# Whole-expert loads in a mixture-of-experts step: one 3 MB load each from the eighth round of three on, with smaller splits around it

## The chip, the core and the metric

The kernel runs on one NeuronCore of one Trainium2 chip. The metric is the device time of one execution in microseconds, as the median of several runs. All data is float32. The engines are TensorE (PE; PEld is its weight load), VectorE (DVE), ScalarE (ACT), GpSimd (POOL) and SyncE (SP), which here does little else than issue DMAs.

## What is computed

Two layers of a backbone over 256 tokens of width 1024: 128 context tokens and 128 latent ones. Each layer has token mixers (retention, differential attention, latent attention), and then a mixture of experts:

```
def trunk_layer(x, cond, lw, ...):
    shift1, scale1, gate1, shift2, scale2, gate2 = split(silu(cond) @ w_ada + b_ada)
    h = rmsnorm(x, norm_mix) * (1 + scale1) + shift1
    x = x + gate1 * (token_mixers(h) @ w_out)
    h = rmsnorm(x, norm_ffn) * (1 + scale2) + shift2
    return x + gate2 * moe_ffn(h)

def moe_ffn(h):    # 64 experts, top 6 of them per token, ff = 256
    eidx, gates = route(sigmoid(h @ router_w) + router_bias)     # grouped top-k
    routed = sum over a token's 6 experts e of gates_e * (silu(h @ w_gate[e]) * (h @ w_up[e])) @ w_down[e]
    return routed + (silu(h @ sh_gate) * (h @ sh_up)) @ sh_down
```

An expert has 2 MB of gate and up weights (each 1 MB) and 1 MB of down weights. Every expert is computed, so both layers read 2 x 64 x 3.1 MB = 403 MB of expert weights.

## The kernel before

**Rounds.** After the mixers of a layer come 22 rounds over the 64 experts: two rounds with two experts each (the fixed ones), then 20 rounds of three, numbered 0 to 19 here (`TRIOS = 20`). "Round r" below is always round of three number r, and the eighth of them is round 7. Experts are sorted by how many tokens chose them; a round has 128 places, 64 for a big expert and 32 for each of two small ones.

**One round on TensorE** (`expert_round`, L2216) in its fixed order: gates and up (L2228, 128 matmuls, waits for `gates_in`), the first half of the gather of the next round's tokens (L2155), the scatter of the previous round's results into the sum in PSUM (L2162), the transposes of hidden values and gated choice (L1642), the second half of the gather, and the down matmuls (L2264, waits for `downs_in`). It counts up `gate_done`, `up_done` and `down_done`. ScalarE copies down results to `yy` in two halves (L1048, `results`). Round 2 has the shared expert's up matmuls in between, round 4 its down matmuls (`sh_down`). In the last round the scatter of round 18's results lies beside the gates and ups, and its own results are scattered behind the downs. VectorE then adds the sum to the residual `xT` (L1610), the norm of the next layer follows.

**Buffers.** Six places for gate and up weights, A, B, C_, D_ (the ring `gu`), F (`fifth`) and S_ (`sixth`, the memory of the hidden tokens), and six for down weights. From round 6 on even rounds use A, B, D_ and odd rounds C_, F, S_, so the loads of round r+2 go where round r's were. The first six rounds have an order of their own (`BUFFERS`, L569).

**Loads** are all issued by SyncE, in program order, on one queue, with waits in between. For round r+2 it reads three expert numbers (`expert_in`), waits for `up_done` of round r, issues the three gate and up loads of 2 MB (L630), waits for `down_done` of round r and issues the three down loads of 1 MB (L633). The last round's gates and ups are six loads of 1 MB (L627). From `trio_loads` (L777), which rounds 6 to 19 use:

```
x = [expert_in(sp, l, at(trio_at(r) + n)) for n in TAKES]
sp.wait_ge(S["up_done"], m * 2 + (r0 + r + 1))
if last: ... load_halves_to(r, js, x, half)
else: load_to(r, js, x)
sp.wait_ge(S["down_done"], m * 2 + (r0 + r + 1))
load_dn_to(r, js, x)
```

In it, r is the round that is loaded, and the counts are those of round r-2. Ahead of it (L774) SyncE waits for `sh_down`, then loads the third down weights of round 5. For rounds 1 and 2 it waits once for `up_done` of round 0 (L738) and issues loads of whole gate and up blocks. The next layer's first weights go into the ring's places as these come free, in an order fixed at L447.

**In HBM** `exp_w_both` holds an expert's gate and up weights as 128 rows of 16 KB, `exp_w_down` its down weights as rows of 8 KB. The residual norm is `norm` (L848 on ScalarE).

## Time and profile before

| | us |
|---|---|
| median of 3 runs (lowest, highest) | 1324.35 (1323.11, 1327.59) |
| the profiled execution, device time | 1323.6 |
| its span, first to last instruction | 1321.7 |
| PE busy | 1218.5 (92%) |
| PE weight loads busy | 835.3 (63%) |
| DVE busy | 280.8 (21%) |
| ACT busy | 239.4 (18%) |
| DMA, mean rate over the span | 376 GB/s |

The page's slices, 40 of 33 us each; a digit is a busy share in tenths, PEclk the granted TensorE clock in tenths of full speed:

```profile
PE   6999999999998898888989999999999888988896
PEclk8999999999998898999999999999999999999999
DMA  9779849999999999999966653999999999999994
GB/s 397 317 311 362 338 181 422 398 427 423 410 424 426 426 427 424 427 427 426 420 266 250 250 225 150 415 417 425 424 397 427 424 428 424 426 427 427 423 423 173
```

Slices 7 to 20 and 26 to 40 are the rounds of the two layers. Times are from the span's start. In the views that follow, an idle time in square brackets stands before an instruction, with what ended it; the chain of waits gives start, duration and what was waited for or ran; a DMA's duration in it is from issue to landing. The view by windows has, for each window, busy time and count of PE, PEld, DVE, ACT and POOL, the granted clock, the DMA share, and GB/s.

### The profile page before, as it was taken

What the parts mean: (1) busy time and instruction counts of PE and PEld (TensorE: products, weight loads), DVE (VectorE), ACT (ScalarE), POOL (GpSimd) and SP (SyncE); (2) the same over time, 40 slices, a digit from 0 to 9 for tenths busy, and PEclk for the clock granted to TensorE, in tenths of its full rate; (3) what the DMA queues carried; (4) which work ended last, traced back from release to release, by engine and by line L of the source; (5) the groups of instructions that cost most, each with busy time, mean ns of one, the idle gap of its engine ahead of it and who ended that gap; (6) DMA issues with size and microseconds to landing.
All of it is one profiled execution on the core that took longest, in us unless ns stands there. A gap on an engine that the chain in (4) does not pass through costs nothing.

```text
span 1321.7 us, 25818 instructions
## 1 busy us (share of the span) xinstructions
PE 1218.5 (92%) x11196; PEld 835.3 (63%) x11196; DVE 280.8 (21%) x720; ACT 239.4 (18%) x533; POOL 2.8 (0%) x13
## 2 busy tenths in 40 slices
PE   6999999999998898888989999999999888988896
PEld 4566687676765565656665658866766564656564
DVE  1252362101011010101034425511111010101012
ACT  2353132101010110000134521411010101100112
POOL 0000000000000000000000000000000000000000
PEclk8999999999998898999999999999999999999999
DMA  9779849999999999999966653999999999999994
GB/s 397 317 311 362 338 181 422 398 427 423 410 424 426 426 427 424 427 427 426 420 266 250 250 225 150 415 417 425 424 397 427 424 428 424 426 427 427 423 423 173
DMA packets 50937, 496.82 MB, mean 376 GB/s; under 512 B 8752, under 2 KB 9008, under 8 KB 10160
## 3 DMA queue, kind: packets, MB, share of 16 engines
q1 hardware_dynamic: 46800, 493.75, 89.8%
q10 hardware_dynamic: 4064, 2.00, 0.5%
q8 instruction: 57, 0.93, 0.3%
q14 instruction: 16, 0.13, 0.0%
HBM read 493.73 MB, written 2.00 MB: 375 GB/s over the span
## 4 chain that ended last, share of the span: by engine, by line
PE 52%; DMA 40%; DVE 3%; SPq 2%; issue 1%; ACT 1%; DVEq 0%; ACTq 0%
DMA xh<-in_exp_w_both 31%; PE PS L2228 16%; PE PS L1732 7%; DMA dn<-in_exp_w_down 4%; PE PS L2064 4%; PE PS L2155 4%; PE PS L2264 4%; PE PS L2162 3%; PE PS L1674 2%; DMA arena<-in_exp_w_both 2%; DMA gu<-in_exp_w_both 2%; PE PS L2113 1%; DMA gu<-in_w_in_wide 1%; PE PS L1642 1%; PE PS L1855 1%
## 5 line engine op out<-in xcount | busy, mean ns | idle before, releaser
L2228 PE MATMUL PS<-gu,arena 128*32 128x256 f32 (+1 forms) x4000 | 334.3, 398 | 72.4 <-DMA gu<-in_exp_w_both 35.2
L2228 PEld LDWEIGHTS PS<-gu,arena 128*32 128x32 f32 (+1 forms) x4000 | 193.7, 116 | 217.5 <-issue 89.2
L2228 PE MATMUL PS<-arena 128*32 128x256 f32 (+1 forms) x768 | 181.8, 397 | 0.0
L2155 PE MATMUL PS<-arena 128*128 128x128 f32 x1408 | 176.3, 278 | 0.5 <-ACT arena L1065 0.5
L2155 PEld LDWEIGHTS PS<-arena 128*128 128x128 f32 x1408 | 164.0, 192 | 18.3 <-issue 17.2
L2264 PE MATMUL PS<-dn,arena 128*32 128x512 f32 (+1 forms) x976 | 160.1, 595 | 2.7 <-DMA dn<-in_exp_w_down 2.7
L2162 PE MATMUL PS<-arena 128*128 128x256 f32 x704 | 160.2, 380 | 1.4 <-ACT arena L1048 1.4
L2264 PE MATMUL PS<-arena 128*32 128x512 f32 (+1 forms) x368 | 152.1, 595 | 0.0
L2162 PEld LDWEIGHTS PS<-arena 128*128 128x128 f32 x704 | 130.2, 190 | 20.7 <-ACT arena L1048 3.2
L2228 PE MATMUL PS<-xh,arena 128*32 128x256 f32 x608 | 139.7, 402 | 0.0
L1558 DVE TENSOR_TENSOR arena<-arena,PS 128x256 f32<-128x256 f32 x44 | 18.5, 422 | 548.3 <-ACT arena L1061 548.3
L1048 ACT ACTIVATE arena<-PS 128x512 f32<-128x512 f32 x88 | 52.6, 597 | 373.5 <-PE PS L2264 373.5
L2264 PEld LDWEIGHTS PS<-dn,arena 128*32 128x32 f32 (+1 forms) x976 | 40.9, 111 | 82.7 <-issue 74.8
L2228 PEld LDWEIGHTS PS<-arena 128*32 128x32 f32 (+1 forms) x768 | 88.6, 117 | 0.0
L1061 ACT ACTIVATE arena<-PS 128x256 f32<-128x256 f32 x44 | 16.9, 384 | 382.8 <-PE PS L2228 382.8
L1552 DVE COPY arena<-PS 128x512 f32<-128x512 f32 x44 | 30.4, 691 | 209.8 <-PE PS L1642 209.8
L2228 PEld LDWEIGHTS PS<-xh,arena 128*32 128x32 f32 x608 | 66.0, 116 | 2.7
L1732 PE MATMUL PS<-gu,xh 128*128 128x512 f32 (+1 forms) x160 | 51.7, 478 | 0.0
L1732 PE MATMUL PS<-xh,gu 128*128 128x256 f32 x192 | 44.6, 392 | 1.8 <-DVE xh L1159 1.8
L1732 PEld LDWEIGHTS PS<-xh,gu 128*128 128x128 f32 x192 | 37.1, 196 | 10.7 <-issue 5.3
L1732 PEld LDWEIGHTS PS<-gu,xh 128*128 128x128 f32 x160 | 26.7, 190 | 21.8 <-issue 21.3
L1674 PE MATMUL PS<-gu,condw 128*32 128x512 f32 x320 | 38.1, 598 | 0.1
(264 smaller groups left out, 1021.7 us busy)
## 6 DMA issues: line engine op xcount, KB each, us to landing
gu<-in_exp_w_both SPq DMA_DIRECT2D x76, 2048.0 KB, 25.4
dn<-in_exp_w_down SPq DMA_DIRECT2D x84, 1024.0 KB, 26.4
arena<-in_exp_w_down SPq DMA_DIRECT2D x44, 1024.0 KB, 27.8
gu<-in_w_ada_pieces SPq DMA_DIRECT2D x20, 2048.0 KB, 8.8
arena<-in_exp_w_both SPq DMA_DIRECT2D x20, 2048.0 KB, 27.7
xh<-in_exp_w_both SPq DMA_DIRECT2D x14, 2048.0 KB, 34.2
gu<-in_exp_w_both SPq DMA_DIRECT2D x20, 1024.0 KB, 14.2
gu<-in_w_in_wide SPq DMA_DIRECT2D x8, 2048.0 KB, 14.2
```

The lines of the kernel that those rows point to most:

```text
L1048: return A(yy[:, :, half], PS[:, 7 - n, :].rearrange("p (t c) -> p c t", c=NC_), ACT.Copy)
L1061: A(sact, PS[:, 5, 0:FF], ACT.Silu).then_inc(S["silu_ready"], 1)
L1552: return v.tensor_copy(turned_back, PS[:, 6, :])
L1558: tt(hh, sact, PS[:, 5, FF:2 * FF], ALU.mult).then_inc(S["hid_ready"], 1)
L1642: return pe.transpose(dst, src, ident[0:parts, 0:parts])
L1674: ins = mmul(PS[32 * j:32 * j + 32, 7, :], condw[:, 2 * quarter + c, :], wv[:, c, 512 * j:512 * j + 512], start=(quarter == 0 and c == 0), ...
L1732: ins = mmul(PS[0:lhs(k).shape[-1], bank, o:o + rhs(k).shape[-1]], lhs(k), rhs(k), start=(k == 0), stop=(k == NC_ - 1))
L2064: ins = mmul(PS[:, wo_bank(c), (c % 2) * T:(c % 2) * T + T], wo[k // 4][:, k % 4, c], mixT[:, k] if k < 4 else latent_T[:, k - 4], start=( ...
L2155: ins = mmul(PS[:, 4, (c % 4) * P:(c % 4) * P + P], h_tok[:, g, c], onehot[b][:, g], start=(g == 0), stop=(g == 1))
L2162: ins = mmul(PS[:, c // 2, (c % 2) * T:(c % 2) * T + T], yy[:, c], selT, start=(first and c % 2 == 0), stop=False, skip_group_check=True)
L2228: ins = mmul(PS[w * h:w * h + w, 5, FF * half:FF * half + FF], xg[:, k, w * h:w * h + w], weights[half][:, k], start=(k == 0), stop=(k == ...
L2264: ins = mmul(PS[w * h:w * h + w, 7 - n, :], hidT[:, j * P + w * h:j * P + w * h + w], weights[:, j, 512 * n:512 * n + 512], start=(j == 0) ...
```

## The change

- Gate, up and down weights of an expert stand together in HBM (`exp_w`, 128 rows of 24 KB), with the down weights in two halves of 512 columns. On the chip each ring place holds gate, up and down weights side by side; F too. `dn` becomes a list of four views of the ring. S_'s down weights use `fourth_dn`, and D_'s from round 6 on the ring's own place.
- `trio_loads`, rounds 7 to 18: an expert is one 3 MB load after `down_done` of round r-2. Only S_, the third of an odd round, keeps a 2 MB load after `up_done` and a 1 MB load.
- Round 6 is written out: its gates are asked for before the waits for `sh_down` and `down_done`, and round 5's third down weights after both.
- Rounds 1 and 2: gate halves after `gate_done` of round 0, up halves after `up_done`.
- The last round: its down weights come in two column halves with a semaphore for each; results go to the scatter and the residual by column halves.
- ScalarE's square root table is asked for ahead of the squares in layer 2 as well; the slots of the next layer's first weights change order.

```diff
-        gu = sb("gu", [P, RING, 2 * NC_ * FF])
-        dn = sb("dn", [P, RING, 2, D])
+        ring = sb("ring", [P, RING, 2 * BLOCK + 2 * D])
+        gu = ring[:, :, 0:2 * BLOCK]
+        OWN = (3, 1, 0, 2)
+        dn = [ring[:, slot, 2 * BLOCK:].rearrange("p (j n) -> p j n", j=2) for slot in OWN]
...
-                    slot = n if l == 0 else expert_slot[l - 1][(0, 1, 3, 2)[n - starts[l]]]
+                    slot = n if l == 0 else expert_slot[l - 1][(3, 0, 1, 2)[n - starts[l]]]
...
+            def load_dn_half(j, l, x, half, told):
+                at = half * D
+                sp.dma_start(dn_place(j)[:, at:at + D], down(l, x)[:, at:at + D]).then_inc(S[told], 16)
+            def load_whole(j, l, x, told):
+                sp.dma_start(fifth_whole if j == F else ring[:, expert_slot[l][j], :], expert(l, x)).then_inc(S[told], 16)
...
-                sp.wait_ge(S["up_done"], r0 + 3)
-                load_to(1, (A,), x1[2:])
-                load_to(2, (B,), x2[:1])
-                load_half(D_, l, x2[1], 0, "even_in")
-                load_fourth_up(l, x2[1], "even_in")
+                for half in range(2):
+                    sp.wait_ge(used[half], r0 + 3)
+                    load_halves_to(1, (A,), x1[2:], half)
+                    load_halves_to(2, (B,), x2[:1], half)
+                    if half == 0:
+                        load_half(D_, l, x2[1], 0, "even_in")
+                    else:
+                        load_fourth_up(l, x2[1], "even_up_in")
...
+                x6 = experts(6, 0, 1, 2)
+                sp.wait_ge(S["up_done"], r0 + 7)
+                load_to(6, (A, B, D_), x6)
                 sp.wait_ge(S["sh_down"], l + 1)
+                sp.wait_ge(S["down_done"], r0 + 7)
                 load_dn_to(5, (S_,), x5[2:])
+                load_dn_to(6, (A, B, LATE_D), x6)
...
+                    if r % 2:
+                        sp.wait_ge(S["up_done"], m * 2 + (r0 + r + 1))
+                        load(S_, l, x[2], "odd_in")
                     sp.wait_ge(S["down_done"], m * 2 + (r0 + r + 1))
-                    load_dn_to(r, js, x)
+                    for j, xj in zip(buffers(r), x):
+                        if j == S_:
+                            load_dn(S_, l, xj, "odd_dn_in")
+                        else:
+                            load_whole(j, l, xj, ("even_in", "odd_in")[r % 2])
+                def last_loads(r):
+                    x = experts(r, 0, 1, 2)
+                    sp.wait_ge(S["up_done"], r0 + r + 1)
+                    for half in range(2):
+                        load_halves_to(r, buffers(r), x, half)
+                    sp.wait_ge(S["down_done"], r0 + r + 1)
+                    for half, told in enumerate(("odd_dn_in", "last_dn_in")):
+                        for j, xj in zip(buffers(r), x):
+                            load_dn_half(j, l, xj, half, told)
...
-                if k % 2:
+                if k > 0:
                     A(small[:, 500:501], col("eps"), ACT.Sqrt)
...
-                    half = slice(64 * n, 64 * n + 64)
-                    return A(yy[:, :, half], PS[:, 7 - n, :].rearrange("p (t c) -> p c t", c=NC_), ACT.Copy)
+                    return A(yy[:, 4 * n:4 * n + 4], PS[:, 7 - n, :].rearrange("p (c t) -> p c t", c=4), ACT.Copy)
...
                     for n in range(2):
+                        if last and n == 1:
+                            pe.wait_ge(S["last_dn_in"], 48 * l + 48)
                         for j in range(2):
                             for h, weights in enumerate(dns):
                                 ins = mmul(PS[w * h:w * h + w, 7 - n, :], hidT[:, j * P + w * h:j * P + w * h + w],
-                                           weights[:, j, 512 * n:512 * n + 512], start=(j == 0), stop=(j == 1))
+                                           by_half(weights)[:, n, j], start=(j == 0), stop=(j == 1))
...
-                pe.wait_ge(S["y_out"], 2 * (r0 + ROUNDS))
-                scatter(told=S["combined"])
+                for half in range(2):
+                    pe.wait_ge(S["y_out"], 2 * (r0 + ROUNDS) - 1 + half)
+                    scatter(told=S["combined"], cs=range(4 * half, 4 * half + 4))
...
+    down = named["exp_w_down"].reshape(DEPTH, E, P, 2, 2, D // 2)
+    named["exp_w_down"] = down.swapaxes(3, 4).reshape(DEPTH, E, P, 2 * D)
+    named["exp_w"] = np.concatenate([named.pop(f"exp_w_{n}").reshape(DEPTH, E, P, 2 * D) for n in ("gate", "up", "down")],
+                                    axis=-1)
```

TensorE's waits follow: an even round from 8 on waits for three whole loads before its gates, an odd one for S_'s gates and two whole loads.

## Rows read from the trace of the kernel before

**Rows 1.** View by windows, two whole rounds of layer 2.
```profile
1072.20:1116.50 44.30, 38.23 (x424) 25.18 (x425) 4.95 (x10) 4.35 (x8) 0.00 (x0) 0.96 1.01 426
```
**Rows 2.** Chain of waits, rounds 15 to 19 of layer 1: start, us, what.
```profile
565.84 8.84 PE PS L2228 x128
...
575.89 34.10 DMA xh<-in_exp_w_both
...
610.12 8.80 PE PS L2228 x128
...
626.59 3.62 PE PS L2264 x32
...
630.36 1.77 SPq L633
...
663.08 3.67 PE PS L2264 x32
```
**Rows 3.** Timeline of PE, from round 18's gates to round 19's, layer 1.
```profile
632.26 7.11 PE L2228 MATMUL PS<-gu,arena 128*32 128x256 f32 x128 [2.10 <-DMA gu<-in_exp_w_both]
...
646.97 0.63 PE L2264 MATMUL PS<-dn,arena 128*32 128x512 f32 x3
...
650.43 0.39 PE L2228 MATMUL PS<-gu,arena 128*32 128x256 f32 x2
```
**Rows 4.** Timeline of PE, the gates of round 8, layer 1.
```profile
410.76 9.97 PE L2228 MATMUL PS<-gu,arena 128*32 128x256 f32 x128 [3.73 <-DMA gu<-in_exp_w_both]
```
**Rows 5.** Last round of layer 2: PE and DVE timelines, then the chain of waits.
```profile
1289.69 0.39 PE L2228 MATMUL PS<-gu,arena 128*32 128x256 f32 x2
...
1301.25 0.69 DVE L1552 COPY arena<-PS 128x512 f32<-128x512 f32 x1 [1.07 <-PE PS L1642]
...
1302.64 0.14 issue
1302.78 3.67 PE PS L2264 x32
...
1307.13 1.15 PE PS L2162 x4
```
**Rows 6.** DMA issues at 197.98, 243.13, 249.69, 250.21: KB each, us to landing.
```profile
arena<-in_exp_w_both SPq DMA_DIRECT2D x1, 2048.0 KB, 14.1
...
arena<-in_exp_w_down SPq DMA_DIRECT2D x1, 1024.0 KB, 8.6
...
gu<-in_exp_w_both SPq DMA_DIRECT2D x1, 2048.0 KB, 7.6
...
gu<-in_exp_w_both SPq DMA_DIRECT2D x1, 2048.0 KB, 13.4
```
**Rows 7.** Windows before an issue at 185.59; that load's landing; the page's y_prompt store.
```profile
180.00:185.50 5.50, 5.50 (x27) 4.85 (x26) 3.43 (x10) 1.05 (x2) 0.00 (x0) 1.00 0.01 1
...
gu<-in_exp_w_both SPq DMA_DIRECT2D x1, 2048.0 KB, 7.7
...
out_y_prompt<-arena ACTq DMA_DIRECT2D x1, 512.0 KB, 3.1
```
**Rows 8.** View by windows, the stretches in which loads run dry.
```profile
245.00:255.00 10.00, 10.00 (x119) 7.63 (x112) 0.42 (x1) 0.98 (x2) 0.00 (x0) 1.00 0.91 352
345.00:350.00 5.00, 5.00 (x49) 2.77 (x52) 2.05 (x4) 0.60 (x1) 0.00 (x0) 1.00 0.98 342
885.00:890.00 5.00, 5.00 (x73) 3.63 (x66) 0.42 (x1) 0.38 (x1) 0.00 (x0) 1.00 1.02 397
980.00:990.00 10.00, 10.00 (x82) 6.80 (x84) 2.05 (x4) 0.99 (x2) 0.00 (x0) 1.00 0.90 337
```
**Rows 9.** Round 8's last down load, issued at 387.98 and at 1027.09.
```profile
arena<-in_exp_w_down SPq DMA_DIRECT2D x1, 1024.0 KB, 30.2
...
arena<-in_exp_w_down SPq DMA_DIRECT2D x1, 1024.0 KB, 30.3
```
**Rows 10.** Start of layer 2: chain of waits, then the timeline of PE.
```profile
673.95 1.28 ACT L861
...
671.63 3.48 PE L1692 MATMUL PS<-xh,cst 128*128 128x256 f32 x13
```

More of the change, by code:

```diff
@@ L566, in trunk @@
         GATHERED, UPPED, TURNED, DOWNED, PE_STEPS = BEFORE + 1, BEFORE + 3, BEFORE + 4, BEFORE + 5, 6
-        A, B, C_, D_, F, S_ = range(6)
+        A, B, C_, D_, F, S_, LATE_D = range(7)
         BUFFERS = ((D_, A, B), (C_, F, A), (B, D_, F), (A, C_, F), (B, D_, A), (C_, F, S_))
@@ L604, in _, with expert @@
         def _(sp):
-            BLOCK = NC_ * FF
+            def expert(l, x):
+                return t["exp_w"][l, bass.ds(x, 1)].rearrange("e p n -> (e p) n")
             def gate_and_up(l, x):
-                return t["exp_w_both"][l, bass.ds(x, 1)].rearrange("e p n -> (e p) n")
+                return expert(l, x)[:, 0:2 * BLOCK]
             def gate_or_up(l, x, half):
-                return t["exp_w_both"][l, bass.ds(x, 1), :, half * BLOCK:(half + 1) * BLOCK].rearrange("e p n -> (e p) n")
+                return expert(l, x)[:, half * BLOCK:(half + 1) * BLOCK]
             def down(l, x):
-                return t["exp_w_down"][l, bass.ds(x, 1)].rearrange("e (p j) n -> (e p) (j n)", j=2)
+                return expert(l, x)[:, 2 * BLOCK:]
             def place(j, l):
@@ L772, in _, with trio_loads @@
                 load_dn_to(5, (C_, F), x5[:2])
+                x6 = experts(6, 0, 1, 2)
+                sp.wait_ge(S["up_done"], r0 + 7)
+                load_to(6, (A, B, D_), x6)
                 sp.wait_ge(S["sh_down"], l + 1)
+                sp.wait_ge(S["down_done"], r0 + 7)
                 load_dn_to(5, (S_,), x5[2:])
-                def trio_loads(m, r, at, last=False):
-                    js = buffers(r)
+                load_dn_to(6, (A, B, LATE_D), x6)
+                def trio_loads(m, r, at):
@@ L781, in trio_loads @@
                     x = [expert_in(sp, l, at(trio_at(r) + n)) for n in TAKES]
-                    sp.wait_ge(S["up_done"], m * 2 + (r0 + r + 1))
-                    if last:
-                        for half in range(2):
-                            load_halves_to(r, js, x, half)
-                    else:
-                        load_to(r, js, x)
-                    sp.wait_ge(S["down_done"], m * 2 + (r0 + r + 1))
-                    load_dn_to(r, js, x)
-                with sp.Fori(0, (TRIOS - UNROLLED) // 2 - 1) as m:
-                    for r in (UNROLLED, UNROLLED + 1):
+                    if r % 2:
+                        sp.wait_ge(S["up_done"], m * 2 + (r0 + r + 1))
+                        load(S_, l, x[2], "odd_in")
@@ L792, in _, with this @@
+                def this(x):
+                    return slice(x, x + 1)
+                trio_loads(0, UNROLLED + 1, this)
+                with sp.Fori(0, (TRIOS - UNROLLED) // 2 - 2) as m:
+                    for r in (UNROLLED + 2, UNROLLED + 3):
                         trio_loads(m, r, lambda x: bass.ds(m * 8 + x, 1))
                 over_loads(sp, l)
-                for r in (TRIOS - 2, TRIOS - 1):
-                    trio_loads(0, r, lambda x: slice(x, x + 1), last=(r == TRIOS - 1))
+                trio_loads(0, TRIOS - 2, this)
@@ L796, in _ @@
+                last_loads(TRIOS - 1)
             sp.wait_ge(S["y_sample"], 1)
@@ L2293, in trio @@
                     gus = [split_fourth if j == D_ and r <= UP_AT else gu_of[j] for j in in_columns(r)]
-                    count = 48 * (turn + 1) + (16 if not odd and r > 0 else 0) + ins_of[odd]
+                    count = 48 * (turn + 1) + ins_of
                     ups = []
-                    if r < 2:
-                        ups = [(S[f"{name}_up_in"], (48, 32)[r] + ups_of[odd])]
+                    if r < 3:
+                        ups = [(S[f"{name}_up_in"], (48, 48, 80)[r] + ups_of[odd])]
                     elif r == TRIOS - 1:
-                        ups = [(S["odd_up_in"], 32 + 48 + ups_of[1])]
-                    expert_round(m if r >= UNROLLED and r < TRIOS - 2 else 0, 2 + r, gus, [dn_of[j] for j in in_columns(r)],
-                                 [(S[f"{name}_in"], m * 48 + count)], ups,
-                                 (S[f"{name}_dn_in"], m * 48 + (48 * (turn + 1) + 48 * TRIOS // 2 * l)), **how)
+                        ups = [(S["odd_up_in"], 48 + 48 + ups_of[1])]
+                    dns = [dn[3] if j == D_ and r >= UNROLLED else dn_of[j] for j in in_columns(r)]
+                    if not odd:
+                        dns_in = (S["even_dn_in"], 48 * min(turn + 1, 4) + 48 * 4 * l)
+                    elif r == TRIOS - 1:
+                        dns_in = (S["odd_dn_in"], ODD_DNS + ODD_DNS * l)
+                    elif r > UNROLLED:
+                        dns_in = (S["odd_dn_in"], m * 16 + (48 * 3 + 16 + ODD_DNS * l))
+                    else:
+                        dns_in = (S["odd_dn_in"], 48 * (turn + 1) + ODD_DNS * l)
+                    expert_round(m if r >= UNROLLED and r < TRIOS - 2 else 0, 2 + r, gus, dns,
+                                 [(S[f"{name}_in"], m * 48 + count)], ups, dns_in, **how)
                 for r in range(UNROLLED):
```

50 lines of the change are left out of this document (26 added, 24 removed).

## The prediction, made before the changed kernel ran

> **What bounds the kernel now.** I read the page's slices first. They show two stretches, the second half of each layer, in which the DMA engines are full while TensorE is nearly full too. So the question is which of the two ends last there. The view by windows gives 426 GB/s over two whole rounds, at a DMA share of 1 [rows 1]: the rounds run at the speed of the loads. The chain of waits says the same, and shows how: it goes from a load's issue to its landing, 34 us later, then at once into the gates of the round that needed it [rows 2]. Two rounds take 44.26 us (the gates at 565.84 and 610.12), so a round takes 22.13 us, in which 9.4 MB land.
>
> Next, how far behind is TensorE? In a round whose matmuls all run at the high clock it needs 18.17 us from its first gate to the first gate of the next (632.26 to 650.43) [rows 3]. Where it has sat idle for 3.7 us or more, the granted clock is at its low level for a part of the gates, and these take 8.8 or 10.0 us in place of 7.11 [rows 2, 4]. I call this extra c. Six such phases in the first layer take 8.4 to 10.1 us, mean 9.35, so c is 2.2 with ends 1.7 and 2.9.
>
> Last, the end of a layer. From the gates of the last round to the copy of the turned hidden values TensorE and its helpers need 12.3 us (1289.69 to 1301.94), and the last down weights land 0.8 us later, at 1302.64 [rows 5]. So the ends of TensorE's work and of the loads nearly coincide today: 18.17 + 12.3 = 30.5 us after the gates of round 18 TensorE is ready for the last down matmuls, and these start after 30.8 us in layer 1 (632.26 to 663.08) [rows 2, 3]. This near tie decides the case.
>
> **Loads in one piece.** Loads of 1 MB in a full queue land every 2.48 us (from 212.1 to 251.7, sixteen of them) [rows 6]. A trio's three loads of 2 MB then take 22.13 - 3 x 2.48 = 14.69, or 4.90 each. Two 1 MB loads take 0.06 us more than one of 2 MB; this is what a load costs beside its bytes. A 3 MB load saves it once: 7.32 us, so 21.96 for an even round's three and 22.02 for an odd round's. Over the 30 loads of a layer this gives 1.8 us. It could be nothing, if a row of 24 KB goes as two packets.
>
> In a full queue the 1 MB loads here run at 423 GB/s [rows 6]. The Trainium skill ("DMA: Bandwidth & Descriptors", Measured) has a lone 1 MB transfer at 78% of peak and 16 MB at 97%, and its fit (Anatomy of one DMA) has 2.0 us fixed per DMA. As an estimate from that page, 60 merged loads would save 120 us. The trace doesn't agree, with 0.06 us each.
>
> **Loads asked for later.** Before, the gates of round r+2 are asked for when the gates of round r are done, 11 us ahead of the end of round r. Now an even round's three loads all wait for the down matmuls of round r. What is still queued then is the load of round r+1. Counting from the landing of round r's loads: gates start at 0.13, downs end at 18.3 + c, the issue follows 0.15 to 0.2 later [rows 2], and the queue ends at 22.02. The lead is 3.5 - c = 1.3 us. What does a lead that short cost? An issue into an idle queue lands 2 MB in 7.7 us, 2.8 over the 4.90 [rows 7]. The trace also has the case of a short lead itself: an issue at 249.69, 2.0 us ahead of the queue's end at 251.7, landed at 257.3, 0.7 late; that is again 2.8 less the lead [rows 6]. The load behind it (263.6) was 2.1 late in all, which makes 4.1. The other end is 1.9 (0.5 MB stored in 3.1 us) [rows 7]. I take 2.8, where two rows meet; the ends are 1.9 and 4.1. So each even round from number 10 on starts 1.5 us late, and as the queue now waits for TensorE, the pair's period is the sum round the loop: 0.13 + 18.17 + c + 0.2 + 2.8 + 21.96 = 43.3 + c = 45.5 us, against 44.26. Odd rounds keep a lead of 5 us and more through the separate 2 MB load of their third gates. TensorE then sits idle about 7 us before an even round (45.5 less two rounds of 18.17 and c), so c comes back every time.
>
> The Trainium skill (same page, Rules for kernel authors) advises issuing a DMA early and waiting late, because the fixed cost then overlaps. This change does the opposite for even rounds. With the 2.0 us of its fit for my 2.8 the sum below would be 8 us less.
>
> **The early edits.** Two stretches per layer in which the loads run dry go away: round three's gate halves are asked for 3.5 us sooner, and the loads of round 6 no longer stand behind the wait for the shared expert's down weights. By the rates of the windows against 426 GB/s [rows 8] these lose 1.7 + 1.0 = 2.7 us in layer 1 and 0.3 + 2.1 = 2.4 in layer 2; the lateness of the first landing alone would give 0.7. The halves add two loads (0.1 us) and the three 3 MB loads of round 8 and two of round 7 save 0.3. Round 8's own loads are asked for at the end of round 6, still some 6 us ahead of the queue's end. The third expert's down weights of round 5 are now asked for at the end of round 4, behind the 14.7 us of loads for round 6's gates, which were asked for 18 us sooner. They land some 12 us later, and TensorE comes to round 5's downs 14.7 us after that round's start (646.97 in [rows 3]): nothing, or under 1 us.
>
> **The end of a layer.** Round 18 now waits for all of its 9.4 MB, its down weights too (7.4 us more of loads ahead of its gates). Behind it only 22 us of loads are left, while TensorE needs 30.5 + c. The last downs and all that hangs on them are no longer bound by the loads but by TensorE.
>
> So per layer, starting from the landing of round 8's down weights (418.2 and 1057.4) [rows 9]:
> Layer 1: 418.2 - 2.7 - 0.2 = 415.3, gates at 415.4, five pairs of 45.5 to round 18: 642.7, then 18.2 + 2.2 + 12.3 = 32.7: 675.4 in place of 663.1: 12.3 late.
> Layer 2: 1057.4 - 2.4 - 0.2 + 0.1 + 227.3 + 32.7 = 1314.9 in place of 1302.8: 12.1 late.
>
> **Column halves and small edits.** The first half's results are evicted while TensorE does the second half's downs, so the scatter starts at the downs' end and not 0.68 us later (1306.45 to 1307.13) [rows 5]: 0.7 saved per layer. The 1.8 us that half of the last downs could hide behind the loads is worth nothing now, as the loads are long in. That is the cover that is gone. Results come in another column order and are copied from consecutive addresses; the ScalarE copy of 0.6 us is off the path in all rounds but the last. The table load for the square root at layer 2's start moves ahead of the squares; before, most of it lay beside the matmuls that add them (they end at 675.1, the table load at 675.2) [rows 10], so 0.1. The new slot order and the interleaved buffers move no bytes more; TensorE reads the same number of columns, at no cost: a conflict would show in 18.17. SyncE's value loads (about 2 us) lie ahead of waits in which it idles. The split of the last downs adds three loads, 0.2 us, hidden.
>
> **Sum.** 12.3 + 12.1 - 1.4 - 0.1 = 22.9 us slower. The profiled execution took 1323.6 (span 1321.7 and 1.9 around it), 0.75 under the median 1324.35. So 1346.5.
>
> **The rivals.**
> Dearer restart: each late issue costs 4.1 and not 2.8, as the second load of the short-lead case says; 1.3 x 5 x 2 = 13 us more, 1359.5. For it: the only rows that show a short lead in full. Against: by then engines had drifted apart over a long full stretch, and here they are lined up anew in each pair.
> Cheap restart, high clock: the restart costs 1.9 and TensorE's clock doesn't fall. Then the lead of 3.5 suffices, the pair takes 44.0, and per layer 415.4 + 219.9 + 30.5 = 665.8, 2.7 late, less 0.7: 1327.6. Against: 7 us idle, where 3.7 were enough to lower the clock. What is left in this case comes from the end alone.
> The other side, faster: a load has a fixed cost even in a full queue that my difference of landing times misses, and each merged load saves s. It acts in the 21.96 of each of the five pairs (15 s) and in the five merged loads ahead of them. It decides from s = 11.5 / 20 = 0.6 us; at s = 1.0 a layer gains 20 less 11.5, and the time is 1307. The rows say 0.06 [rows 6], and 3 MB in 6.3 us would be 500 GB/s, where the windows hold 426 [rows 1]. The fixed cost of the Trainium skill's fit, above, is a rule of this kind.
>
> **Chances.** Forecast 0.66 (own range 1334 to 1358), dearer restart 0.17, cheap restart 0.10, faster 0.07. The ends of c and of the restart together would give 1331 and 1372; both at one end at once is unlikely. The range is 1328 to 1363, with about 0.1 left out on each side. A difference under 0.3% (1320.4 to 1328.3) can't be told from none; most of the cheap restart lies there. Faster 0.07, same 0.07, slower 0.86.
>
> **What would show it.** Right: in the rounds from 10 on the even gates wait about 7 us for a load and the odd ones not at all; gates at 45.5 us per pair; windows of 5 us below 400 GB/s once per pair; the last downs of a layer start with no wait for a load, 32.7 us after round 18's gates; even gate phases of 8.8 to 10 us. Wrong: pairs at 44.0 and full windows (restart hidden); a last down that waits for the loads (round 18's gates came earlier than I say); 3 MB landing in clearly under 7.3 us.

## The result, and the profile after

| | before | after |
|---|---|---|
| median | 1324.99 us (4 runs) | 1354.07 us (4 runs) |
| profiled execution, span | 1321.7 us | 1351.7 us |
| mean granted TensorE clock | 0.977 | 0.955 |

The ratio is 1.0224, with a 95% interval from 1.0208 to 1.0240. The changed kernel is 29.1 us slower; the forecast was 22.2 slower than the median (1346.5 against 1324.35), and its range of 1328 to 1363 holds the result.

The page of the changed kernel: the span, the slices (PE's busy share, the granted clock, what the DMA engines moved) and the 3 MB loads into the ring; twelve more go into F.
```profile
span 1351.7 us, 25651 instructions
...
PE   7999999999988779778999999999998879778877
...
PEclk9999999999989899889899999999999999889889
...
GB/s 400 326 318 322 350 221 420 419 426 423 427 430 388 432 408 391 411 416 408 416 153 275 240 244 152 419 420 423 427 424 426 431 390 408 407 416 419 385 418 71
...
ring<-in_exp_w SPq DMA_DIRECT2D x48, 3072.0 KB, 18.7
```
In the second half of each layer the slices now swing between 385 and 432 GB/s. Before they stood at 420 to 428.

Windows of the changed kernel, each as long as a pair of rounds, in layer 1, and a short one (columns as in [rows 1]):
```profile
420.70:466.80 46.10, 38.94 (x452) 25.38 (x448) 4.94 (x10) 4.35 (x8) 0.00 (x0) 0.93 0.95 400
466.80:512.90 46.10, 37.05 (x408) 24.68 (x404) 4.94 (x10) 4.35 (x8) 0.00 (x0) 0.89 0.99 417
512.90:559.00 46.10, 38.59 (x420) 24.73 (x415) 4.95 (x10) 4.35 (x8) 0.00 (x0) 0.89 0.95 400
...
525.00:530.00 5.00, 5.00 (x76) 2.37 (x72) 0.00 (x0) 1.19 (x2) 0.00 (x0) 1.00 0.51 157
```
A pair lasts 46.1 us on average (45.3 to 47.1) in place of 44.26. The last row is where the time goes: around the late issue at 527.65 the DMA engines work half of the time, at 157 GB/s. TensorE is busy for about as long as before, 37 to 39 us a pair against 38.2.

The chain of waits of the changed kernel, rounds 14 to 19 of layer 1, to be laid beside [rows 2]:
```profile
574.22 0.04 SPq L647
...
575.40 23.86 DMA ring<-in_exp_w
...
599.31 8.91 PE PS L2268 x128
...
615.89 3.62 PE PS L2306 x32
...
620.71 24.53 DMA ring<-in_exp_w
...
645.38 9.76 PE PS L2268 x128
...
662.81 3.57 PE PS L2306 x32
...
677.75 0.70 DVE arena L1588
...
678.50 3.64 PE PS L2306 x32
```
Before, this chain ran 34 us through a load and then into gates. Now it goes round a loop: down matmuls (L2306), issue (L647), 24 us until the third 3 MB load lands, gates (L2268), and again down matmuls. After round 18's gates it is TensorE's and its helpers' work alone, to the last downs at 678.50: no load in it.

How the 30.0 us between the two spans are made up, in times counted from a layer's first expert gates. Before and after, these start at 208.84 and 207.68 in layer 1, and at 847.36 and 861.03 in layer 2:

| us | forecast, layers 1 and 2 | layer 1 | layer 2 |
|---|---|---|---|
| round 8's gates | 206.6, 207.5 | 207.4 | 208.8 |
| five pairs, round 8 to 18 | 227.3 | 230.3 | 230.4 |
| round 18's gates to last downs | 32.7 | 33.1 | 33.4 |
| last downs, from first gates | 466.6, 467.5 | 470.8 | 472.6 |
| the same, before | | 454.2 | 455.4 |

So the layers grow by 16.6 and 17.2 us. The part ahead of the experts was 1.2 us shorter, which is chance: in the kernels below the first gates start anywhere from 206.0 to 211.8. From layer 1's last downs to layer 2's first gates it was 1.8 shorter, and from the last downs to the end 0.8.

### The profile page after: what moved, and what is told of

Read it like the earlier page. It is cut to its first block, busy times and chain, and to the rows that moved or that the text cites. A ratio compares the mean times of both kernels' runs of the same rounds, so it can differ in the third digit from the quotient of the medians.

```text
span 1351.7 us, 25651 instructions
## 1 busy us (share of the span) xinstructions
PE 1223.7 (91%) x11196; PEld 829.4 (61%) x11196; DVE 280.8 (21%) x720; ACT 239.4 (18%) x534; POOL 2.8 (0%) x13
## 4 chain that ended last, share of the span: by engine, by line
PE 68%; DMA 26%; DVE 3%; issue 1%; SPq 1%; ACT 0%; DVEq 0%; ACTq 0%
DMA ring<-in_exp_w 24%; PE PS L2268 19%; PE PS L2191 8%; PE PS L2306 8%; PE PS L2198 7%; PE PS L1768 7%; PE PS L2100 4%; PE PS L1710 2%; PE PS L1678 2%; PE PS L2149 1%; PE PS L1891 1%; PE PS L1902 1%; PE PS L2240 1%; DMA arena<-in_exp_w 1%; PE PS L1999 1%
## 5 line engine op out<-in xcount | busy, mean ns | idle before, releaser
L2268 PE MATMUL PS<-ring,arena 128*32 128x256 f32 (+1 forms) x4000 | 342.9, 413 | 100.2 <-DMA ring<-in_exp_w 90.3
L2268 PEld LDWEIGHTS PS<-ring,arena 128*32 128x32 f32 (+1 forms) x4000 | 189.6, 120 | 256.1 <-issue 82.1
L2268 PE MATMUL PS<-arena 128*32 128x256 f32 (+1 forms) x768 | 175.2, 387 | 0.0
L2191 PEld LDWEIGHTS PS<-arena 128*128 128x128 f32 x1408 | 164.0, 192 | 18.3 <-issue 17.2
L2306 PE MATMUL PS<-ring,arena 128*32 128x512 f32 (+1 forms) x960 | 159.9, 595 | 1.6 <-DVE arena L1588 1.6
L2268 PE MATMUL PS<-xh,arena 128*32 128x256 f32 x608 | 133.1, 389 | 0.0
L2306 PE MATMUL PS<-arena 128*32 128x512 f32 (+1 forms) x384 | 101.6, 595 | 0.0
L2306 PEld LDWEIGHTS PS<-ring,arena 128*32 128x32 f32 (+1 forms) x960 | 39.9, 111 | 81.9 <-issue 75.1
L2268 PEld LDWEIGHTS PS<-arena 128*32 128x32 f32 (+1 forms) x768 | 87.2, 114 | 0.0
L2268 PEld LDWEIGHTS PS<-xh,arena 128*32 128x32 f32 x608 | 64.8, 113 | 2.7
L1768 PE MATMUL PS<-ring,xh 128*128 128x512 f32 (+1 forms) x160 | 51.7, 478 | 0.0
L1768 PE MATMUL PS<-xh,ring 128*128 128x256 f32 x192 | 43.7, 384 | 1.7 <-DVE xh L1195 1.7
L1768 PEld LDWEIGHTS PS<-xh,ring 128*128 128x128 f32 x192 | 35.6, 190 | 11.3 <-issue 6.6
L1768 PEld LDWEIGHTS PS<-ring,xh 128*128 128x128 f32 x160 | 26.7, 190 | 21.8 <-issue 21.3
L1710 PE MATMUL PS<-ring,condw 128*32 128x512 f32 x320 | 38.1, 598 | 1.3 <-DMA ring<-in_w_ada_pieces 1.3
```

What stands on the lines that cost most here:

```text
L1710: ins = mmul(PS[32 * j:32 * j + 32, 7, :], condw[:, 2 * quarter + c, :], wv[:, c, 512 * j:512 * j + 512], start=(quarter == 0 and c == 0), ...
L1768: ins = mmul(PS[0:lhs(k).shape[-1], bank, o:o + rhs(k).shape[-1]], lhs(k), rhs(k), start=(k == 0), stop=(k == NC_ - 1))
L2191: ins = mmul(PS[:, 4, (c % 4) * P:(c % 4) * P + P], h_tok[:, g, c], onehot[b][:, g], start=(g == 0), stop=(g == 1))
L2268: ins = mmul(PS[w * h:w * h + w, 5, FF * half:FF * half + FF], xg[:, k, w * h:w * h + w], weights[half][:, k], start=(k == 0), stop=(k == ...
L2306: ins = mmul(PS[w * h:w * h + w, 7 - n, :], hidT[:, j * P + w * h:j * P + w * h + w], by_half(weights)[:, n, j], start=(j == 0), stop=(j = ...
```

## The experiments

Two theories stood against each other at first: that the late asking in even rounds and the order at the layer's end each cost time, as predicted, or that something else in the change does (the 24 KB rows, a load of 3 MB in itself). The kernels are the changed one with the edits shown. The diffs show their main lines; the counts that TensorE waits for follow. The medians of the kernel before were 1323.2 to 1323.5 in these comparisons.

**All loads apart.**
```diff
-                    if r % 2:
-                        sp.wait_ge(S["up_done"], m * 2 + (r0 + r + 1))
-                        load(S_, l, x[2], "odd_in")
+                    sp.wait_ge(S["up_done"], m * 2 + (r0 + r + 1))
+                    for j, xj in zip(js, x):
+                        load(j, l, xj, names[0])
                     sp.wait_ge(S["down_done"], m * 2 + (r0 + r + 1))
-                    ...
-                            load_whole(j, l, xj, ("even_in", "odd_in")[r % 2])
+                    for j, xj in zip(js, x):
+                        load_dn(LATE_D if j == D_ else j, l, xj, names[1])
```


> The changed kernel, but each expert of rounds 7 to 18 again comes in two loads: 2 MB asked for when the gates two rounds earlier are done, 1 MB when the downs are. The joined rows in memory, the early edits, the column halves and the slot order stay. Theory (the loss is the late asking and round 18's down weights ahead of its gates): rounds of 22.1 us again, pairs 44.2 to 44.3, layer 1's last downs at 663.1 less 2.7 and less the 1.2 that the dense part gained, near 659; 1317 us in all (range 1314 to 1321). Rival A (the joined 24 KB rows or another edit that stays is dear): above 1330. Rival B (a load costs something even in a full queue, so that merging helps): pairs above 44.5.


Measured: 1320.71 us, ratio 0.9977 (0.9964 to 0.9990). Pairs take 44.28 us (429.06 to 606.18, four of them), the last downs of layer 1 come at 660.33, and the time is in the theory's range. So the whole loss lies in the joined loads of rounds 7 to 18 and in when they are asked for. The joined rows in memory cost nothing that shows: rival A is out.

**Each cure alone.** First, round 18's three experts are loaded in two parts again. Second, in even rounds only expert D is.
```diff
+                    apart = (A, B, D_,) if r == TRIOS - 2 else ((), (S_,))[r % 2]
```


> The changed kernel, but round 18's three experts come in 2 MB and 1 MB, asked for early and late as before; rounds 10 to 16 keep their late 3 MB loads. Theory: four late restarts of 2.0 us a layer stay (pairs 46.1 against 44.1), the last pair falls to about 44 and the last downs follow round 18's gates by about 30.8 us in place of 33.1, started some 7 us earlier: a layer 10 to 11 us shorter than in the changed kernel, 1333 us (1329 to 1338). Rival (the restarts are nearly all of the loss, the end costs little): one restart less per layer, 1350 us.


Measured: 1334.31 us, ratio 1.0083 (1.0058 to 1.0109).
```diff
+                    apart = () if r == TRIOS - 2 else ((D_,), (S_,))[r % 2]
```


> The changed kernel, but in even rounds one of the three experts (the wide one's third place, D) comes in 2 MB asked for with the gates two rounds earlier, and 1 MB later; the other two stay at 3 MB, asked for after the downs; round 18 stays whole. The queue is then 4.9 us longer when the 3 MB loads are asked for. Theory (a short lead is what costs in the rounds): pairs at 44.0 to 44.2 in place of 46.1, ten pairs save 20 us, and the gates of round 18 come another 2 or so earlier against their loads only if these were the wait: 1333 us (1329 to 1337). Rival A (3 MB loads themselves slow the rounds): pairs stay near 46, 1352. Rival B (TensorE's low clock sets the pair, not the lead): pairs stay above 45.5.


Measured: 1331.93 us, ratio 1.0061 (1.0040 to 1.0082). Windows of this second kernel over two pairs:
```profile
477.30:521.30 44.00, 38.35 (x424) 26.01 (x425) 4.95 (x10) 4.35 (x8) 0.00 (x0) 0.96 1.01 429
521.30:565.30 44.00, 38.42 (x427) 26.07 (x428) 4.94 (x10) 4.35 (x8) 0.00 (x0) 0.96 1.01 429
```
3 MB loads, 6 of an even round's 9 MB still asked for late, and the pair is 44.0 us at 429 GB/s: it isn't the size of the loads, nor the low clock by itself (odd rounds' gates of 8.8 us at a granted clock of 0.81 stand in these pairs too), but how long the queue still is at the late issue. Here it is 5.8 us and more. Both times are near their forecast of 1333.

**Both cures.**
```diff
+                    apart = (A, B, D_,) if r == TRIOS - 2 else ((D_,), (S_,))[r % 2]
```


> The two cures together: in even rounds 8 to 16 expert D comes in 2 MB (early) and 1 MB (late) and the other two at 3 MB; round 18's three all come in two loads, asked for early and late. Odd rounds, early edits and column halves are those of the changed kernel. Theory (lead and layer end are separate terms that add): pairs of 44.1, the last downs some 32 us after round 18's gates, which come 6 to 7 us sooner than in the kernel with one expert ahead alone: 1318 us (1315 to 1321), at or a little under the 1320.7 of all loads apart. Rival (the two cures overlap, since the round before 18 is bound by something else): 1326 or more.


Measured: 1321.29 us, ratio 0.9979 (0.9966 to 0.9993), just outside the range. From the ratios, in us of 1323.2: the change costs 32.4 over this kernel, the late issues alone 13.8 (round 18 apart) and the end alone 10.9 (one ahead). Together they cost 7.7 more than their sum, a figure on which the intervals of the four ratios leave some 5 us of doubt. About 4 of these would be a late issue that both cures remove, that of round 18 itself; what the rest is, no run shows.

**The cost of a lead, in more doses.** Half as much of expert D is asked for early, 1 MB (its gate half).
```diff
+                    else:
+                        sp.wait_ge(S["gate_done"], m * 2 + (r0 + r + 1))
+                        load_half(D_, l, x[2], 0, "even_in")
...
```
The other 2 MB of D still come late.


> The changed kernel, but in even rounds from 8 on the gate half (1 MB) of expert D is asked for when the gates two rounds earlier are done, and its other 2 MB late with the rest; round 18 too. The queue is then 2.5 us longer at the late issue: a lead of 4.0 us in place of 1.5. The trace of the changed kernel, of the kernel with round 18 apart and of the two filled ones has these costs (spacing of the first landing less 7.31): 2.6 to 3.4 us at a lead of about -0.4 to 0.5, 1.1 to 3.3 at 1.3 to 2.1, 0 to 1.9 at 2.9 to 3.4, none at 5.8 and more. Theory (the cost is a restart less the lead): 0 to 0.6 at 4.0, pairs of 44.0 to 44.6, 1336 us (1333 to 1341). Rival (the cost hangs on how many loads are taken out of the early group, not on the queue's length): pairs above 45, 1345 or more.


Measured: 1333.19 us, ratio 1.0072 (1.0052 to 1.0093), at the low end of the theory's range. Its profiled execution was the longest of its runs (1339.96), and five of its ten late issues lost 0.5 to 2.3 us there, five nothing.

Then the cause doubled: in odd rounds, too, all loads wait for the downs.
```diff
+                    sp.wait_ge(S["down_done"], m * 2 + (r0 + r + 1))
                     if r % 2:
-                        sp.wait_ge(S["up_done"], m * 2 + (r0 + r + 1))
                         load(S_, l, x[2], "odd_in")
-                    sp.wait_ge(S["down_done"], m * 2 + (r0 + r + 1))
```


> The cause doubled: in odd rounds the separate 2 MB load too waits for the down matmuls, so that from round 7 on every round's loads are asked for late, not every second round's. Theory of the loop (a round's loads can't be asked for before the downs of the round two before it; 0.13 + 18.17 + c + 0.2 + restart 3.6 + 22.0 us for two rounds): two rounds still take 44.1 + c = 44.1 to 46.1, and the time stays at 1346 to 1356. Rival (each late issue costs its own 2 us): pairs of 48, 1374 us.


Measured: 1353.07 us, ratio 1.0218 (1.0195 to 1.0242), the same as the change (1.0224). Twice as many late issues cost nothing more. It is a loop: when an even round starts late, the odd round's issue, a round later, has a lead of 6 us again (5.9 to 8.0 in the trace from round 11 on).

The late issues of 3 MB loads in the changed kernel and ten of the experiments, by how long after the issue the last of the loads already queued landed (lead), and how much later than 7.31 us after that load the first new one landed:

| lead, us | issues | loss, us: least, mean, most |
|---|---|---|
| -0.5 to 0.8 | 15 | 2.1, 2.8, 4.0 |
| 0.8 to 2.2 | 23 | 0.9, 1.9, 3.3 |
| 2.2 to 3.2 | 7 | 0.0, 0.7, 2.3 |
| 3.2 to 4.4 | 14 | 0.0, 0.6, 1.9 |
| 4.4 to 8.0 | 20 | -0.1, 0.0, 0.4 |

Three issues into an empty queue landed 10.2 to 11.1 us later (these in the two filled kernels, below), 2.9 to 3.8 over 7.31.

Two rows of the DMA issues show how much is lost. First the changed kernel, the issue at 574.37, when 0.6 us was queued: 10.2 - 0.6 - 7.3 = 2.3 lost.
```profile
ring<-in_exp_w SPq DMA_DIRECT2D x1, 3072.0 KB, 10.2
```
Then the kernel filled less, below, the issue at 525.14, when 3.0 us was queued: nothing lost, though this load took as long from issue to landing.
```profile
ring<-in_exp_w SPq DMA_DIRECT2D x1, 3072.0 KB, 10.3
```
With the queue just empty the loss is 2.8 us on average, which is the value that the prediction took from the idle queue [rows 7]. But a lead of 1.6 us doesn't take 1.6 off: 1.9 is left, not 1.2. The losses scatter by more than 1 us at the same lead, and only beyond 4.4 us is nothing lost, but for one 0.4.

A lead in landings isn't what the DMA engines still have to do. Around the changed kernel's issue at 527.65, with a lead of 1.7 us:
```profile
526.00:528.60 2.60, 2.60 (x44) 1.21 (x40) 0.00 (x0) 0.98 (x2) 0.00 (x0) 1.00 0.08 35
528.60:530.60 2.00, 2.00 (x44) 1.23 (x40) 0.00 (x0) 0.00 (x0) 0.00 (x0) 1.00 1.14 344
```
The engines are all but idle from 526.0 on, 3.3 us ahead of the last landing (529.31), and work again 1.0 us after the issue: here the two make the 4.3 us that a lead would have had to be. It isn't so at each issue. At 480.26 (lead 2.1) the engines' share never fell under 0.9, and still the first load landed 3.1 us late.

**TensorE's clock in the loop.** Matmuls that nothing reads, ahead of even rounds' gates.
```diff
+                    if u >= 2 + UNROLLED and u % 2 == 0:
+                        for k in range(46):
+                            mmul(PS[:, 5, 0:P], h_tok[:, 0, k % NC_], onehot[b][:, 0], start=True, stop=True)
```


> The changed kernel with 46 matmuls of 128x128 by 128x128 that nothing reads ahead of the gates of each even round from 8 on, in the time in which TensorE waits for a load (0.125 us each, 5.8 us in all, of 7 to 9 us). They keep TensorE's clock up. Theory (the pair's period goes round a loop: 43.3 + c and more of restart, c being the low clock's extra): even gate phases fall from 8.4-10 us to 7.1-7.5, pairs from 46.1 to about 44.1, the last downs follow round 18's gates by 31 us in place of 33.1: 2 us at twelve places, 1331 us (1328 to 1340). Rival (the loads alone set the pair, and a TensorE phase that ends sooner only waits longer): 1352 us.


In `u` the two fixed rounds are counted too, so the first of these matmuls stand ahead of round 6, and not of round 8 as was meant.

Measured: 1383.35 us, ratio 1.0449 (1.0428 to 1.0471). Its chain of waits (L2265 are the fillers, L2271 the gates):
```profile
459.23 10.47 PE PS L2265 x92
469.69 7.04 PE PS L2271 x128
...
506.12 10.47 PE PS L2265 x92
```
The gates take 7.1 us at the high clock, as expected, but 46 calls are 92 instructions and 10.5 us, more than the wait of 7 to 9. The fill became the bound. With 28 calls:

> The changed kernel with the fill of the first trial cut from 46 to 28 matmuls, because each ran as two instructions and took 0.23 us, so that 46 took 10.6 us, longer than TensorE's wait: its pairs of 46.9 were TensorE's own work. Now 28 take 6.4 us of the 7 to 9 us of waiting. Theory (the low clock's extra c is in the loop from landing to issue): even gate phases 7.1, pairs 46.1 less 2 = 44.1 to 44.5, the last downs 31 us after round 18's gates, 1331 us (1328 to 1340). Rival (the pair doesn't hang on TensorE's speed): 1352.


Measured: 1350.26 us, ratio 1.0210 (1.0188 to 1.0233). The windows of its pairs:
```profile
416.40:462.20 45.80, 43.16 (x480) 31.45 (x480) 4.94 (x10) 4.35 (x8) 0.00 (x0) 1.00 0.99 418
462.20:506.60 44.40, 43.11 (x483) 31.48 (x483) 4.94 (x10) 4.35 (x8) 0.00 (x0) 1.00 0.99 417
506.60:550.40 43.80, 43.02 (x481) 31.43 (x480) 4.95 (x10) 4.35 (x8) 0.00 (x0) 1.00 1.00 423
```
And its chain of waits at round 18:
```profile
631.88 0.53 PE PS L2265 x3
632.40 4.14 issue
636.54 7.81 PE PS L2265 x53
644.35 7.04 PE PS L2271 x128
```
With a granted clock of 1.00 the pairs shrink from 46.1 to between 43.9 and 45.8: the clock's extra is in the loop, as predicted. (A part of it is that the shorter gates lengthen the lead to 3 us.) The forecast of 1331 was missed by 19 us all the same, in two places. The last pair of a layer took 49.9 us (594.39 to 644.28, and 1249.09 to 1299.04), where the four before it took 44.5 and 44.8 on average: 10.6 us in the two layers. And round 8's gates came 3.0 and 4.0 us later after the first gates than in the changed kernel: the fillers ahead of round 6, whose gates had no wait there to hide them, moved the issue of round 8's loads so far back that its lead fell from 7.3 and 5.6 us to 0.3 and -1.2.

The last four rows show the last pair. At round 18 TensorE stands still for 4.1 us among the fillers, while nothing in the chain holds it ("issue"), and the round's gates start 5 us after its loads have landed (639.3). This is the first pass through the code behind the loop over rounds. The DMA queues in this stall (632.4 to 636.5) show what else went on:
```profile
q1 hardware_dynamic: 69, 1.70, 97.0%
q8 instruction: 1, 0.02, 1.4%
```
A packet of 16 KB on the queue that the profile calls instruction ran from 634.0 to 634.9; in the loop, from 400 on, that queue had carried none. The same holds for each of the sixteen stalls of this kind, in eight kernels: the first such packet in 221 to 249 us starts between 1.8 us ahead of the stall and 3.0 after its start, and TensorE goes on 1.3 to 1.7 us after the packet's end. So the stall is very likely TensorE's wait for its next instructions, though the trace doesn't say for which engine a packet is. In the changed kernel the packet came at 639.7, inside the wait for round 18's loads (637.61 to 645.38), which hid it.

**The clock at the end.** The same trick where it should pay, in the kernel with both cures: 12 calls ahead of odd rounds' gates.
```diff
+                    if u > 2 + UNROLLED and u % 2 and not last:
+                        for k in range(12):
...
```


> The kernel with both cures, and 12 matmuls of 128x128 that nothing reads (two instructions each, 0.11 us each, 2.7 us in all) ahead of the gates of odd rounds 7 to 17, inside the 3.7 us in which TensorE waits. In the kernel with both cures round 17's gates take 8.80 us and round 18's 8.86, and the end of the layer is bound by TensorE. Theory: with the clock kept up both take 7.1, the last downs of a layer come 3.4 us sooner, 6.8 in all: 1314.5 us (1312 to 1318). Rival (the loads bind the end as soon as TensorE is faster, or the clock falls all the same): 1319 to 1322.


Measured: 1325.91 us, ratio 1.0016 (1.0003 to 1.0028), slower than both cures without it. What TensorE waited for in the gates of round 18, in layer 1 of the kernel with both cures:
```profile
PE PS L2274 <- issue: 1.2, 1, 1.2
```
And in layer 1 and layer 2 of this one:
```profile
PE PS L2277 <- issue: 2.3, 1, 2.3
...
PE PS L2277 <- issue: 4.4, 1, 4.4
```
My reading of round 18's 8.86 us in the kernel with both cures was wrong. It isn't the low clock: the granted clock is 1.00 there, and 1.2 of the 1.75 us over 7.11 are the same stall. In layer 1 the longer stall took away what the fill had gained in round 17 (last downs 455.2 and 455.3 us after the first gates). In layer 2 it took 3.1 more: it came ahead of the gates, and these then ran at a granted clock of 0.72, in 9.8 us. The other kernels whose round 18 doesn't wait for loads show it too, in each layer: 0.7 to 2.0 us long without a fill (five kernels), 0.9 to 5.6 with one (three).

**The small edits.** The early edits undone, and the column halves of the last downs and scatter undone, both in the kernel with both cures.
```diff
+                sp.wait_ge(S["up_done"], r0 + 3)
                 for half in range(2):
-                    sp.wait_ge(used[half], r0 + 3)
...
+                sp.wait_ge(S["sh_down"], l + 1)
                 sp.wait_ge(S["up_done"], r0 + 7)
                 load_to(6, (A, B, D_), x6)
-                sp.wait_ge(S["sh_down"], l + 1)
```


> The kernel with both cures, with the early edits undone: round 3's gate halves are asked for together with its up halves, and round 6's gate and up loads wait for the shared expert's down matmuls. The prediction gave these edits 2.7 and 2.4 us: 5.1 slower than with both cures, 1323. Rival A (the queue has slack later, and only the lateness of the first landings counts): 0.7 slower. Rival B (what is saved early is given back, as round 18's end is bound by TensorE): no difference.


Measured: 1323.35 us, ratio 1.0000 (0.9987 to 1.0013). The time is the forecast's, but by luck: it is 2.1 us over both cures, with intervals that overlap, and 5.1 was expected. The windows with the early edits:
```profile
240.00:270.00 30.00, 30.00 (x368) 18.87 (x370) 4.52 (x9) 3.37 (x6) 0.00 (x0) 1.00 1.01 419
330.00:360.00 30.00, 30.00 (x334) 21.75 (x327) 2.47 (x5) 2.31 (x5) 0.00 (x0) 1.00 1.01 426
```
And without:
```profile
240.00:270.00 30.00, 30.00 (x371) 19.92 (x368) 2.90 (x6) 3.87 (x8) 0.00 (x0) 1.00 0.97 396
330.00:360.00 30.00, 30.00 (x291) 22.48 (x281) 2.89 (x6) 3.15 (x6) 0.00 (x0) 1.00 0.99 409
```
The early edits fill the dry stretches, and by the rates this is 30 x 23/426 + 30 x 17/426 = 2.8 us in layer 1, as predicted. Round 7's gates come 1.9 and 2.1 us sooner in the two layers, counted from the first gates. But round 8's come only 0.7 sooner in both: with the edits one of its or round 7's 3 MB loads lands 8.6 and 8.8 us after the load before it, without them 7.3. In eight kernels with the early edits and 3 MB loads one such landing stands there in both layers (8.0 to 8.8).

The instruction queue has a part in it. Over all kernels with 3 MB loads, 523 of these were issued with 6 us or more of loads ahead of them. Of the 463 with no 16 KB instruction packet between the landing before and their own none came more than 0.2 us late; of the 60 with one, 24 came 0.4 to 1.6 us late, and the landings above are among them. Why the other 36 weren't late stays open, and so does why the kernel without the early edits, which has the packet there too (410.5), was spared.
```diff
-                    for half, told in enumerate(("odd_dn_in", "last_dn_in")):
-                        ...
+                    load_dn_to(r, buffers(r), x)
...
-                for half in range(2):
-                    pe.wait_ge(S["y_out"], 2 * (r0 + ROUNDS) - 1 + half)
-                    scatter(told=S["combined"], cs=range(4 * half, 4 * half + 4))
+                pe.wait_ge(S["y_out"], 2 * (r0 + ROUNDS))
+                scatter(told=S["combined"])
```


> The kernel with both cures, with the last round's down weights in one load each and the last scatter after both halves of the results. Theory: in this kernel too the last downs wait for TensorE's own chain and not for loads, so only the overlap of eviction and scatter goes: 0.7 a layer, 1.4 us slower. Rival (the loads still bind at the end, and the halves hide part of the last downs): up to 2.5 a layer, 3 to 5 us slower.


Measured: 1321.88 us, ratio 0.9986 (0.9976 to 0.9996). What TensorE waits for at the end of layer 2 without the halves; with them the row of the scatter (L2202) is gone:
```profile
PE PS L2308 <- DVE arena L1592: 0.8, 1, 0.8
PE PS L2202 <- ACT arena L1088: 0.7, 1, 0.7
```
The 0.7 us is there in the trace; the medians, 0.6 us apart with intervals that overlap, can't tell it. The last downs wait for a copy and not for loads, so the halves hide nothing more.

**A version faster than the kernel before.** Both cures, with odd rounds' loads apart as well.
```diff
+                    apart = (A, B, D_,) if r == TRIOS - 2 else ((D_,), (C_, F, S_,))[r % 2]
```


> The kernel with both cures, and all three experts of odd rounds 7 to 17 in 2 MB and 1 MB again; only experts A and B of rounds 8 to 16 still come in one 3 MB load. In the kernel with both cures the gates of round 17 wait for 3 MB loads and start 403.24 us after the layer's first expert gates (615.06 - 211.82), with all loads apart 399.80 (606.18 - 206.38); the last downs follow at 455.32 and 453.95. The pairs take 43.99 and 44.28 us. Theory (the end of a layer hangs on how early round 17's and 18's gates can start, so down weights ahead of round 17's gates cost a little of what they save): round 17's gates near 399.3, the last downs 453.4, some 2 us a layer less than with both cures, 1318 us (1316 to 1321). Rival (the pairs alone decide, and more merged loads are better): 1322 or more.


Measured: 1318.09 us, ratio 0.9962 (0.9949 to 0.9976), 5.0 us faster than before; against both cures it is 2.2 us by the ratios, with intervals that overlap. Pairs take 44.13 us and the last downs of layer 1 come 452.80 us after the first gates (659.27 - 206.47), as expected. But the theory's reason failed: round 17's gates were expected at 399.3 and came at 402.6, close to the 403.2 of both cures. They wait for no load: round 16's gates run at the low clock (9.92 us), and TensorE is what sets them. What the layer gains over both cures comes behind this point: round 17's gates run at the high clock (7.1 us against 8.8), and the stall in round 18 is shorter (0.7 against 1.2).
```profile
565.70 22.33 DMA ring<-in_exp_w
...
588.07 9.92 PE PS L2274 x128
...
609.23 6.91 PE PS L2274 x128
...
659.27 3.64 PE PS L2312 x32
```

## Why the prediction was right, and where it was off

- **Loads set the rounds before; a loop does after.** Right. Even gates wait 6.8 to 9.1 us for a load from round 10 on, odd ones not at all, and the kernel with everything asked for late has nearly the same pair (45.7 and 45.9 us): the loop, not the number of late issues.
- **3 MB loads save 0.06 us each.** Right. They land every 7.30 to 7.32 us in a full queue, and the pair with four joined loads takes 43.99 us (439.10 to 615.06, four pairs) against 44.28 with none: 0.07 each. With this the faster case, a hidden cost of every load, is out. The fixed cost of the Trainium skill's fit ("DMA: Bandwidth & Descriptors", Anatomy of one DMA), which the page gives for DMAs issued by GpSimd and not by SyncE, doesn't show between queued loads in these runs either.
- **The restart.** This is the term that was mis-sized. The prediction let each late issue cost 2.8 us less the lead: 1.5 a pair. The ten of the changed kernel have leads of 0.6 to 2.1, mean 1.55, and lose 2.0 on average. 2.8 is right at a lead of zero, but a lead of 1.6 takes off 0.9 only. In the terms of the loop, the first load lands 3.6 us over 7.31 after its issue on average, and not 2.8. Pairs of 46.1 against 45.5 make 3.0 us in each layer. The dearer case, 4.1, was no nearer: it needed 1.3 more in each pair, and 0.6 came. What was said against it, that the engines are lined up anew in each pair, doesn't hold either: in the changed kernel from 432 to 436, with a load still to land at 436.98, their share is 0.41.
- **The other half of the restart.** A late issue in five loses a further 0.7 to 0.9 us at its third load (619.67 and 1274.74, those of round 18). The prediction's short-lead row [rows 6] had shown such a second delay, from which it made the 4.1. In all three places a 16 KB packet of the instruction queue lies ahead of the late landing (639.7, 1294.6, and 261.5 before): so it need not be a part of the restart.
- **The low clock comes back each time.** Right: even phases of 8.4 to 10.0 us, and 7.1 where TensorE is kept busy. The size, c = 2.2, fits: from even gates to the late issue it takes 19.8 to 21.3 us, mean 20.4, against 18.17 + 2.2 + 0.2.
- **The layer's end is TensorE's.** Right: the last downs come 33.1 and 33.4 us after round 18's gates, forecast 32.7, after a wait of 0.8 us for a copy and not for loads. Alone the late end is worth 10.9 us in the two layers.
- **Early edits, 2.7 and 2.4 us.** The dry stretches went, as said. But of this only 0.7 a layer reached round 8's gates in the kernel with both cures, and round 8's gates of the changed kernel came 0.8 and 1.3 us later than forecast. This is the second mis-sized term: about 1 us a layer.
- **Column halves, 0.7 a layer, and nothing from the cover.** Right by the trace; the medians are too coarse for it.
- **The sum.** Later than forecast by 0.8 + 3.0 + 0.4 in layer 1 and 1.3 + 3.1 + 0.7 in layer 2, 9.3 us. Against this 1.2 us of chance ahead of the first gates and 1.1 between and behind the layers. 22.9 became 30.0 by the spans. By the total alone the forecast (22.9 slower) and the dearer restart (35.9) can't be told apart, since 29.1 lies midway; the pairs and the end of the layer have to be read.

The Trainium skill's advice ("DMA: Bandwidth & Descriptors", Rules for kernel authors) to issue early and wait late is borne out: here early means a lead of 4.4 us or more.

## What to carry to other kernels

Where loads bound the kernel, a joined load is worth only what a load costs in a full queue (0.06 us here), and it costs the earlier of its two issue points. Look at how many microseconds of loads are still queued when each late issue comes; under about 4 the queue loses time, and which engine then sets the period is a loop to be added up, not a share of busy time. And a whole load ahead of the last gates of a stage moves its down weights ahead of them: ask whether that stage's end then waits for loads or for the engine.

## What was not expected of the hardware

- The loss of a short lead isn't "restart less lead": on average 2.8 us at 0.1, 1.9 at 1.6, 0.6 at 3.6, none from 4.4 on, with a scatter of a microsecond or more at the same lead. Why two issues with a lead of 3.0 lose 0.0 and 2.3 stays open.
- TensorE stands still for 0.7 to 5.6 us in its first pass through the code behind a loop, with a 16 KB packet on the instruction queue in or just ahead of each stall. A wait for loads at that place hides it; a kernel that removes this wait meets it.
- A 3 MB load in a full queue landed late, by up to 1.6 us, only where such a packet ran meanwhile (24 of 60); of the 463 others none was more than 0.2 us late.
- The stall can look like the low clock, as a phase of 8.86 us in place of 7.11. The granted clock of the stretch tells the two apart.
